# Second block's mixing: rotation tables built during the second MLP, state chunks in step with heads, one root for each group of the mix norm

## The reference, cut to what matters

```python
def stick_breaking_attention(q, k, v):            # 8 heads of 64, blocks of 128 queries
    z = einsum('bhqd,bhkd->bhqk', qb, kh) * scale
    log_1mb = where(mask, log_sigmoid(-z), 0.0)
    later = lax.cumsum(log_1mb, axis=3, reverse=True) - log_1mb
    w = where(mask, exp(log_sigmoid(z) + later), 0.0)
    return einsum('bhqk,bhkd->bhqd', w, vh)

def s5_ssm(u, ...):                               # 256 channels, 1024 complex states
    x[l] = a * x[l-1] + (B u)[l]                  # complex a = mag * (cos + i sin)
    y = Re(C x) + d * u
    ya, yb = split(y @ glu_w)
    return ya * sigmoid(yb)

g = branch_norm_g
mixed = concatenate([rms_norm_2(o_sb, g[:512]), rms_norm_2(o_conv, g[512:768]),
                     rms_norm_2(o_ssm, g[768:])], axis=-1)
x = x + mixed @ w_out                             # rms_norm_2: x * rsqrt(mean(x*x) + 1e-6) * g
```

## Time and profile before

| | us |
|---|---|
| median of 3 runs | 2764.59 |
| lowest, highest | 2762.73, 2766.24 |
| profiled execution | 2760.31 |
| its span | 2758.5 |

### The profile page before, as it was taken

The page is one execution under the profiler, slowest core; times in us unless marked ns, Lnnn a source line. Parts: engine busy times, 40 slices in busy tenths (PEclk is TensorE's granted clock), DMA queues, the critical chain, the costliest instruction groups (busy, mean ns, idle before and its releaser), DMA issues.

```text
span 2758.5 us, 31907 instructions
## 1 busy us (share of the span) xinstructions
PE 2454.7 (89%) x11622; PEld 1975.0 (72%) x11622; DVE 1513.6 (55%) x2034; ACT 956.7 (35%) x1494; POOL 1125.4 (41%) x843
## 2 busy tenths in 40 slices
PE   5999768899999997679989999897878788899999
PEld 5888657788888886556768888676534465688887
DVE  6756756755555544988552122479379444452523
ACT  3312222512121224457552233443333343432322
POOL 1433003344444432358634444345764131344444
PEclk6999879999999998889999999999989899999999
DMA  5333103232333331321122323132200020232323
GB/s 223 115 102 127 39 8 115 84 114 101 112 111 102 114 99 39 102 54 41 56 77 92 99 92 96 62 108 84 92 0 0 31 73 27 69 107 91 99 92 107
DMA packets 68821, 231.68 MB, mean 84 GB/s; under 512 B 8048, under 2 KB 10992, under 8 KB 68592
## 3 DMA queue, kind: packets, MB, share of 16 engines
q1 hardware_dynamic: 68720, 230.35, 25.8%
HBM read 219.57 MB, written 2.10 MB: 80 GB/s over the span
## 4 chain that ended last, share of the span: by engine, by line
PE 57%; issue 15%; DVE 13%; POOL 10%; ACT 3%; DMA 1%; SPq 0%; POOLq 0%; DVEq 0%; ACTq 0%
PE PS L640 41%; POOL HL L517 9%; PE PS L658 6%; DVE RD L2242 2%; PE PS L677 1%; PE PS L609 1%; PE PS L901 1%; DVE ZZ L2396 1%; DVE SM L2226 1%; PE PS L1160 1%; PE PS L783 1%; PE PS L1042 1%; PE PS L1077 1%; DVE STATE L2081 1%; PE PS L786 1%
## 5 line engine op out<-in xcount | busy, mean ns | idle before, releaser
L517 POOL TENSOR_TENSOR HL<-RAW,HL 128x512 fp32r<-128x512 f32 x614 | 905.0, 1497 | 1502.3 <-ACT HL L1205 1502.0
L640 PE MATMUL PS<-HA,HL 128*128 128x512 f32 (+1 forms) x2592 | 557.3, 368 | 18.3 <-DVE V L2007 5.1
L640 PE MATMUL PS<-HID,HL 128*128 128x512 f32 (+1 forms) x2832 | 565.6, 362 | 0.0
L640 PE MATMUL PS<-HB,HL 128*128 128x512 f32 (+1 forms) x2592 | 542.8, 362 | 0.0
L640 PEld LDWEIGHTS PS<-HID,HL 128*128 128x128 f32 x2832 | 478.8, 188 | 85.4
L640 PEld LDWEIGHTS PS<-HA,HL 128*128 128x128 f32 x2592 | 444.4, 190 | 111.4 <-issue 32.3
L640 PEld LDWEIGHTS PS<-HB,HL 128*128 128x128 f32 x2592 | 442.8, 189 | 77.5
L1205 ACT ACTIVATE HL<-RAW 128x1024 fp32r<-128x1024 f32 x307 | 323.0, 1053 | 495.5 <-PE PS L640 385.5
L1859 DVE CUSTOM_DVE_ANT_0 ADJ<-ADA,CB 128x1024 f32<-128x1024 f32 x160 | 267.8, 1674 | 8.8 <-DVE X L1781 2.7
L1781 DVE SCALAR_TENSOR_TENSOR X<-PS,MOD,X 128x256 f32<-128x256 f32 (+1 forms) x120 | 75.7, 658 | 335.2 <-PE PS L640 317.1
L658 PE MATMUL PS<-HA,HL 128*128 128x256 f32 (+1 forms) x576 | 136.1, 399 | 69.6 <-DVE HA L1762 49.2
(11 more groups left out here) (372 smaller groups left out, 2779.1 us busy)
## 6 DMA issues: line engine op xcount, KB each, us to landing
RAW<-wstream SPq DMA_DIRECT2D x307, 512.0 KB, 3.5
ADA<-adastream SPq DMA_DIRECT2D x80, 512.0 KB, 3.6
EARLY<-adastream SPq DMA_DIRECT2D x16, 512.0 KB, 14.4
QB<-QH SPq DMA_DIRECT2D x32, 128.0 KB, 2.3
X<-x_in SPq DMA_DIRECT2D x8, 384.0 KB, 6.8
QC<-QL SPq DMA_DIRECT2D x16, 128.0 KB, 2.3
out<-X SPq DMA_DIRECT2D x8, 256.0 KB, 2.3
X<-mem SPq DMA_DIRECT2D x1, 1024.0 KB, 12.3
```

The costliest lines, as they stand in the source:

```text
L517: a = pool.tensor_tensor(HL[:, t % RING, 1, half], RAW[:, t % RAW_RING, half], HL[:, t % RING, 0, half].bitcast(F32), ALU.subtract)
L640: mm = pe.matmul(bank(t % 2, r), w[:, wp, k * P:(k + 1) * P], a[:, ap, lo:hi], start=(k == 0 and (wp, ap) == (0, 0)), stop=(k == nk - 1 an ...
```

## The change

Four things change. The tables are built in 14 pieces between 14 weight splits of the second MLP, from tile `T_TURNS` on, in memory that is free by then; only the first turning still waits for `T_OUT2`. VectorE runs `state(h)` in head h, and TensorE the output of chunk h-1. In the close each group of the norm is summed and rooted when its own chunks are there: the convolution's first, then the attention's, then the state space's, whose sums TensorE makes within the pair, before chunk 6. Group 2 uses bank 7, and the gate's four products go to banks 7, 0, 2, 6. The square of the root is made by ScalarE; the gain (with its factor -0.5/n, multiplied in once before the second block) goes into VectorE's scaling, so that ScalarE only copies the rounded half. `TB` has four buffers, and the pair takes the chunks in the order of `MIX_ORDER`.

```diff
+T_TURNS = T_U2 - 24
...
-        TA = sb("TA", [P, 2, NX], offset=arena + 28672)
-        TB = sb("TB", [P, 2, NX], offset=arena + 32768)
+        TB = sb("TB", [P, 4, NX], offset=arena + 28672)
...
-        TC = sb("TC", [P, KC, P], offset=ha_at)
-        TS_ = sb("TS_", [P, KC, P], offset=ha_at + 4096)
+        TC = sb("TC", [P, KC, P], offset=cb_at)
+        TS_ = sb("TS_", [P, KC, P], offset=cb_at + 4096)
...
+        MIX_BANK = [4, 5, 7]
+        GATE_BANK, VALUE_BANK = [7, 2], [0, 6]
...
-            lows(T_OUT1 + AHEAD, T_OUT2 + AHEAD)
+            lows(T_OUT1 + AHEAD, T_TURNS)
...
-            pool.wait_ge(S("tile_done"), T_OUT2)
...
+            pool.wait_ge(S("att_low"), ATT_HEADS // 2)
...
+            for i in range(7):
+                turn_products(2 ** i)
+                low(T_TURNS + 2 * i)
+                turn_sums(2 ** i)
+                low(T_TURNS + 2 * i + 1)
             pool.sem_inc(S("turns_ready"), 1)
+            lows(T_TURNS + 14, T_OUT2 + AHEAD)
...
                     pool.wait_ge(S("bt_ready"), 4)
+                    pool.wait_ge(S("tile_done"), T_OUT2)
...
-                if h >= 2:
-                    state_out(h - 2)
+                if h:
+                    state_out(h - 1)
...
-            state_out(6)
-            state_out(7)
...
-            for k in range(6):
+            for k in range(5):
                 mix_sum(k)
-
-            pe.wait_ge(S("y_read"), 2)
-            for m in (2, 0, 3, 1):
...
+            state_out(7)
+            mix_sum(5)
...
+            pe.wait_ge(S("y_read"), 2)
+            pe.wait_ge(S("sb_weights"), 4 * SB_HEADS)
             pe.wait_ge(S("sb_out"), 4)
+            for c in range(2):
+                glu(GATE_BANK[c], 2 + c)
+                glu(VALUE_BANK[c], c)
+
+            def mix_ready(m):
+                if m == 6:
+                    pe.wait_ge(S("glu_exp"), 1)
+                    mix_sum(6)
+                    mix_sum(7)
+                pe.wait_ge(S("mix_lo"), MIX_ORDER.index(m) + 1)
+
+            gemm_pair(t, "x", H, ready=mix_ready, order=MIX_ORDER)
...
+            def mix_root(g):
+                act.wait_ge(S("mix_sum"), (2, 6, 8)[g])
+                act.activation(RSG[:, g, :], PS[:, MIX_BANK[g], :], ACT.Ln, scale=1.0 / MIX_DIM[g],
+                               bias=EPSC[:, 0:1]).then_inc(S("mix_rsqrt"), 1)
+                act.wait_ge(S("mix_rsqrt"), 3 * g + 1)
+                act.activation(RSG[:, g, :], RSG[:, g, :], ACT.Exp, scale=-0.5).then_inc(S("mix_rsqrt"), 1)
+                act.wait_ge(S("mix_rsqrt"), 3 * g + 2)
+                act.activation(NTM[:, g, :], RSG[:, g, :], ACT.Square).then_inc(S("mix_rsqrt"), 1)
...
+            for k in range(4):
+                mix_square(k)
+            act.wait_ge(S("sb_summed"), SB_HEADS)
+            mix_root(0)
+            mix_square(4)
+            mix_square(5)
+            mix_high(0)
+            mix_high(1)
+            gate(0)
+            mix_root(1)
+            gate(1)
+            mix_high(2)
+            mix_high(3)
+            mix_square(6)
+            mix_high(4)
+            mix_high(5)
+            mix_square(7)
+            mix_root(2)
+            mix_high(6)
+            mix_high(7)
...
+            for lo, hi, n in ((0, 4, 512), (4, 8, 256)):
+                a = dve.tensor_scalar(pc(PC["brg"] + lo, hi - lo), pc(PC["brg"] + lo, hi - lo), -0.5 / n, None, ALU.mult)
+            link(a)
...
-                if h:
-                    state(h - 1)
-                if h == 5:
+                state(h)
+                if h == 4:
                     state_y(0)
...
+            def mix_root(g):
+                n = MIX_DIM[g]
+                dve.wait_ge(S("mix_rsqrt"), 3 * g + 3)
+                link(dve.scalar_tensor_tensor(NTM[:, g, :], PS[:, MIX_BANK[g], :], n * EPS, NTM[:, g, :], ALU.add, ALU.mult))
+                link(dve.scalar_tensor_tensor(RSG[:, g, :], NTM[:, g, :], 3.0 * n, RSG[:, g, :], ALU.subtract, ALU.mult))
...
+            mix_root(0)
+            mix_scale(0)
+            mix_scale(1)
+            state_y(1)
+            mix_low(0)
+            mix_low(1)
+            gate(0)
+            mix_root(1)
+            mix_scale(2)
+            mix_scale(3)
+            mix_low(2)
+            gate(1)
+            mix_low(3)
+            mix_scale(4)
+            mix_scale(5)
+            mix_low(4)
+            mix_low(5)
             dve.wait_ge(S("glu_out"), 2)
...
+            mix_root(2)
+            mix_scale(6)
+            mix_scale(7)
+            mix_low(6)
             mix_low(7)
```

More of the change, by code:

```diff
@@ L548, in tt, with turn_products @@
                 return pool.tensor_tensor(out, a, b, op)
[L550 to L557 removed]
+            def turn_products(wide):
                 wc = prm(R_W7C).unsqueeze(2).to_broadcast([P, KC, wide])
@@ L560, in _, with turn_sums @@
                 c0, s0 = TC[:, :, 0:wide], TS_[:, :, 0:wide]
[L561 to L568 removed]
+                tt(TC[:, :, wide:2 * wide], c0, wc, ALU.mult)
+                tt(PX[:, 0, :, 0:wide], s0, ws, ALU.mult)
+                tt(TS_[:, :, wide:2 * wide], s0, wc, ALU.mult)
+                link(tt(PX[:, 1, :, 0:wide], c0, ws, ALU.mult))
+            def turn_sums(wide):
+                c1, s1 = TC[:, :, wide:2 * wide], TS_[:, :, wide:2 * wide]
+                tt(c1, c1, PX[:, 0, :, 0:wide], ALU.subtract)
+                link(tt(s1, s1, PX[:, 1, :, 0:wide], ALU.add))
                 tt(prm(R_T0), prm(R_W7C), prm(R_W7C), ALU.mult)
@@ L1622, in mix_square @@
                 act.activation(SQM[:, k % 2, :], mix_source(k), ACT.Square).then_inc(S("mix_square"), 1)
-            for k in range(6):
-                mix_square(k)
-            for c in range(2):
-                act.wait_ge(S("glu_done"), 2 * c + 1)
-                act.activation(GT[:, c, :], PS[:, 2 + c, :], ACT.Exp, scale=-1.0).then_inc(S("glu_exp"), 1)
-            for k in (6, 7):
-                mix_square(k)
-            for g in range(3):
-                act.wait_ge(S("mix_sum"), (2, 6, 8)[g])
-                a = act.activation(RSG[:, g, :], PS[:, 4 + g, :], ACT.Ln, scale=1.0 / MIX_DIM[g], bias=EPSC[:, 0:1])
@@ new lines, in mix_high, with gate @@
+            def mix_high(k):
+                act.wait_ge(S("mix_scaled"), k + 1)
+                act.activation(H(MIX_ORDER[k])[:, 0, NCTX:NT], TB[:, k % 4, :], ACT.Copy).then_inc(S("mix_hi"), 1)
+            def gate(c):
+                act.wait_ge(S("glu_done"), 2 * c + 1)
+                act.activation(GT[:, c, :], PS[:, GATE_BANK[c], :], ACT.Exp, scale=-1.0).then_inc(S("glu_exp"), 1)
+            for k in range(4):
+                mix_square(k)
+            act.wait_ge(S("sb_summed"), SB_HEADS)
@@ L2441, in _, with mix_scale, mix_low, gate @@
             dve.tensor_copy(QS[:, 3, :], PS[:, 6, :]).then_inc(S("sb_out"), 1)
-            state(7)
-            state_y(1)
-            for c in range(2):
+            def mix_root(g):
[3 more added lines that the diff above has]
+                link(dve.scalar_tensor_tensor(RSG[:, g, :], NTM[:, g, :], 3.0 * n, RSG[:, g, :], ALU.subtract, ALU.mult))
+            def mix_scale(k):
+                if k >= 4:
+                    dve.wait_ge(S("mix_hi"), k - 3)
+                    dve.wait_ge(S("mix_lo"), k - 3)
+                dve.scalar_tensor_tensor(TB[:, k % 4, :], mix_source(k), pc(PC["brg"] + MIX_ORDER[k]),
+                                         RSG[:, MIX_GROUP[k], :], ALU.mult, ALU.mult).then_inc(S("mix_scaled"), 1)
+            def mix_low(k):
+                m = MIX_ORDER[k]
+                dve.wait_ge(S("mix_hi"), k + 1)
+                dve.tensor_tensor(H(m)[:, 1, NCTX:NT], TB[:, k % 4, :], H(m)[:, 0, NCTX:NT].bitcast(F32),
+                                  ALU.subtract).then_inc(S("mix_lo"), 1)
+            def gate(c):
                 dve.wait_ge(S("glu_exp"), c + 1)
```

68 lines of the change are left out of this document (13 added, 55 removed).

## The result

The changed kernel takes **2731.9 us** in the median of 4 runs (2726.93 to 2742.69), the kernel before, timed beside it, 2765.4 (2762.73 to 2768.55). The ratio is 0.9885, 95% interval 0.9858 to 0.9912: 33.5 us less, where 27.1 were forecast. The forecast of 2737.5 has the right side and lies 5.6 above; the measured median is 0.1 us under the low end of the range.

| us | before | forecast | after | after, second profile |
|---|---|---|---|---|
| softplus 0 to softplus 1 | 27.39 | 17.0 | 17.01 | 17.03 |
| softplus 0 to 2 | 45.43 | 33.9 | 34.02 | 35.34 |
| softplus 0 to the end E of the last values matmul | 142.99 | 133.0 | 131.27 | 138.99 |
| E to the end of the first pair of output tiles | 60.38 | 43.3 | 44.24 | 43.03 |
| both together, called the stage below | 203.37 | 176.3 | 175.51 | 182.02 |

What follows compares the result with a forecast made beforehand. The prediction took the stage to be set by three waits: tables, heads and close, with TensorE not full there. Gains of 10.0 us to the last values matmul and 17.1 in the close make 27.1: 2764.59 to 2737.5, range 2732 to 2748.

Steps and rivals of the forecast that it cites:

- Tables into the MLP, cost 0: Second MLP: 26.8 us of table pieces fit between 14 weight splits, which leave 40.8 us; cost 0.
- The fourth rival: Second MLP: splits starve TensorE; sign turns at 79 us of pieces, 2792 us at four times their length; chance 0.03.
- Softplus 1 and 2: Heads 0 and 1: softplus 1 comes 10.4 us earlier, softplus 2 11.5 us earlier.
- The other heads: Heads after softplus 2: 1.5 us given back, so the last values matmul ends 10.0 us earlier.
- the half microsecond in four heads: Heads 1, 3, 5, 6: turning starts 0.5 us earlier and shares the first rotation step; +0.5 each, bounds 0 and 1.0.
- the order of the path is unchanged: Heads 2 to 7: output matmuls still read a chunk finished just before that head's softplus, so path order stays.
- The lock rule: Heads: shared-port lock blocks a rotation's first step fully, 1.0 not 0.5 in four heads; total gain 25.1 instead of 27.1.
- The close: From the last values matmul to the first output pair's end: 43.3 us, 17.1 less; bounds E+40.8 and E+48.
- The mixture of levels: Close: matmuls after a gap priced by the pair's own row, 8.46 us for 24 against 5.60 at the higher level.
- Rival 2: Close runs at TensorE's lower level, pair ends at E+48 to E+50; gain 20 to 22.4, about 2743.5 us; chance 0.17.
- rival 1: Heads 1 to 6 wait for their turning or lose the first rotation step; 8 us less gained, 2745.5 us; chance 0.13.
- Rival 3: Close: VectorE's waits for ScalarE's copies chain, E+50 to E+53; gain 17 to 20, 2746 us; chance 0.07.

Runs made afterwards that it cites:

- run 10: Also written pieces2: changed kernel with every table piece issued twice; stretch holding the second MLP 417.9 us against the changed kernel's 405.4; no total time given.
- Run 7: Changed kernel with four of GpSimd's six turning steps per chunk left out, so it computes something else; 2707.6 us in one run.
- run 11: Also written gate_exp: awake_close with both gates wholly on ScalarE, VectorE's addition and reciprocal removed; 2726.6 us, ratio 0.9875.
- runs 8 and 9: Changed kernel with unread matmuls keeping TensorE busy: 8 in close and heads 0, 2, 4, 6, 2722.4 us; 9 in the close only, 2731.0 us.
- heads: Kernel before with the tables in the second MLP and chunks in step with the heads, but the old close; 2740.7 us, ratio 0.9911.
- awake_close: Changed kernel with unread matmuls only in the close, three before chunk 1 and six before chunk 6; 2731.0 us in one run.
- square_dve: Changed kernel with the square of each group's root made by VectorE instead of ScalarE; 2724.6 us in one run.
- after_again: Changed kernel itself, unchanged, run and profiled again in the third batch beside the kernel before; 2731.8 us, ratio 0.9898.

## Why the prediction was right, and where it was not

- **Tables into the MLP, cost 0: right, the lateness behind it wrong.** TensorE keeps 2.72 us a group, and the stretch is 405.4 us against 404.3, within the scatter of the kernels. But one split came 5.0 us late where the sum had 1.9 and the free room was given as 3.7. The sum spread the splits evenly, one in 5.44 us; where ScalarE's copies come 2.1 us apart (1677.13 and 1679.23) two splits are due together, and the sums' piece between them took 4.84 us, not 3.5. What held was the cover of 11.3 us behind it. The fourth rival's arithmetic failed: by its pool of 76.2 + 11.3 us, pieces of up to 52 us cost nothing and the sign turns at 79; at twice the pieces 12.5 us were lost (run 10). Where the sign turns was not measured.
- **Softplus 1 and 2: right to 0.1 us**, 10.4 and 11.4 us earlier (10.4 and 11.5).
- **The other heads: in part right, the sum by luck.** From softplus 2 to 7 the prediction gives back 1.5 us; the kernel after gives back 3.8, its second profile 6.0. The term is the half microsecond in four heads. The traces don't show one more shared step in each of those heads: in heads 0 to 6 of the kernel after three, six, two, six, three, six and one of the six rotation steps are shared. What made up for it is the tail: the trace of before has a slow group (3.78 + 5.59) before its end and takes 11.48 us from softplus 7 to E, the first profile after 7.36, the second 11.58. So E came 11.7 us earlier instead of 10.0, in the second profile 4.0. The step that failed is "the order of the path is unchanged": it is, but the fully shared rotation ends late, the output matmuls behind it wait 3.4 us and more, and TensorE's clock falls in some of them. The prediction weighed that level for the close alone. The lock rule of the Trainium skill (SBUF — State Buffer, section "SBUF: two separate sides") would have had 25.1; the profiles have 27.9 and 21.4, and don't decide between it and 27.1. Run 7 agrees with the rule itself: 0.69 against 1.46 to 1.75 for the same step.
- **The close: right, 44.2 and 43.0 for 43.3**, with the predicted second reciprocal late (run 11: 2.9 us) and the predicted gap before chunk 6 (5.80). The mixture of levels taken there was right in size: all at the higher level is 40.2 (runs 8 and 9), forecast E+40.8. Rival 2 happened in part, and so did rival 1: no scan waits for a turning, but in heads 1, 3 and 5 the first rotation step is lengthened too (1.49 us in head 1, not 0.69). Rival 3 did not.
- **Credit.** The prediction gives 10.0 to the tables with the heads and 17.1 to the close. The runs share it otherwise: tables 17.0, regrouped close 7.9 on top, the step between +2.9 and -3.6, each from one profile a kernel. The sum came out since it followed the timeline; the parts overlap, because what takes chunk 7 out of the close costs the heads.
- **The 6.4 us beyond the forecast** (33.5 against 27.1) are no term of it. 7.4 us of the profiled difference were there at 1350, before any changed instruction ran, and 5.9 at softplus 0. In seven profiles that hold the whole change softplus 0 starts between 1978.4 and 1988.0, in the two of before at 1986.6 and 1986.8. In the third batch the gain was 28.1. Whether the change has a part in the head start, and why TensorE, always busy at a granted clock of 1.00, takes 134.9 or 136.8 us for 16 tiles of the first MLP, stays open.

## What to carry to other kernels

Fill a square before giving credit: a part that moves work from one stretch to the next looks good in the stretch that it leaves. When tables or other side work go between the steps of a full stream, compare the largest piece with the slack of its own slot as the trace shows it, not the sum with the spare time: the slots are not all alike. Where TensorE waits for another engine on the path, price the matmuls behind the wait at both levels, in every head, and take a second profile. Where two engines slow each other, look at when their steps meet: an earlier start of one can cost more than it gives.

## What the runs showed that I had not expected

- Matmuls that nobody reads shorten the close by 2.8 to 4.0 us although they are 8 us of added work (2.73 and 5.31): the granted clock of that stretch goes from 0.85 to 1.00. In the heads it is open what the same trick brings (130.9 against 131.3 or 139.0).
- One kernel has two patterns of heads, 131.3 and 139.0 us, and the slower one follows the faster head 0. Of seven profiles whose instructions in the heads are those of the kernel after, five lie at 131.1 to 133.8 (after, heads, awake_close, square_dve, pieces2) and two at 137.8 and 139.0 (gate_exp, after_again). Both with the old step and the tables in the MLP lie at 126.5.
- How much goes with four of GpSimd's six steps a chunk: 15 us in the heads, TensorE's level included, though VectorE's scans never wait for GpSimd there.
